# Two blocks of a transformer in one launch on one core: splits, waits and products reordered around three norms and at the last product

## The reference, cut to what matters

```python
x = x + hier_moe(rms_norm(x, ffn_norm), ...)           # 64 experts, top 2
h = rms_norm(x, final_norm)
xn = rmsnorm(h, pre_mix_norm)
rq, rk, rv, rg, cq, ckv, kr = split(xn @ w_in)
ret_out = silu(rg) * head_groupnorm(retention(rope(rq), rope(rk), rv), ret_gn_w)
q = rmsnorm(cq, mla_q_norm) @ w_uq; k, v = rmsnorm(ckv, mla_kv_norm) @ w_ukv   # MLA, 8 heads
mix = concat([ret_out, mla_causal(q, k, v)]) @ w_o
h = h + rmsnorm(mix, post_mix_norm)
ff = (silu(hn @ w_gate) * (hn @ w_up)) @ w_down        # hn = rmsnorm(h, pre_ffn_norm)
h = h + rmsnorm(ff, post_ffn_norm)
h = h + rmsnorm(p @ w_ple_proj, ple_norm) * sigmoid(h @ w_ple_gate + b_ple_gate)
```

## Time and profile before

| what | value |
|---|---|
| median of 3 runs | 2030.41 us (2029.95 to 2030.84) |
| the profiled execution, own time | 2028.34 us |
| its span | 2026.5 us |
| mean granted TensorE clock | 0.953 |
| PE, DVE, ACT, POOL busy | 87%, 45%, 32%, 13% |
| chain that ended last, by engine | PE 61%, DMA 28%, DVE 5%, ACT 2% |

### The profile page before, as it was taken

How to read it: one execution, slowest core, us unless ns; L and a number is a source line. 1 busy time by engine, 2 the same in 40 slices (tenths; PEclk the granted TensorE clock), 3 DMA queues, 4 the chain that set the end, 5 groups by cost and what they waited for, 6 DMA issues and landing times.

```text
span 2026.5 us, 37712 instructions
## 1 busy us (share of the span) xinstructions
PE 1758.4 (87%) x15176; PEld 1247.5 (62%) x15176; DVE 921.1 (45%) x1747; ACT 641.8 (32%) x1256; POOL 271.7 (13%) x285
## 2 busy tenths in 40 slices
PE   7999999887787787778778777789989899999998
PEld 5677788644343343434334343468867799998877
DVE  5455435332322232232223223375375698886245
ACT  4444522421111111111111111143365654445143
POOL 0000000000000000000000000640010078880000
PEclk9999999898998898898889889999999999999999
DMA  6222323799999999999999999943230233333222
GB/s 210 79 84 64 93 93 138 282 419 419 424 427 425 425 427 423 427 424 426 426 425 425 424 427 425 420 131 104 79 95 1 74 104 116 105 105 118 100 84 83
DMA packets 107012, 505.69 MB, mean 250 GB/s; under 512 B 7272, under 2 KB 56808, under 8 KB 73904
## 3 DMA queue, kind: packets, MB, share of 16 engines
q1 hardware_dynamic: 101184, 492.07, 61.0%
q10 hardware_dynamic: 3856, 7.74, 1.4%
q0 software_dynamic: 1888, 4.70, 0.9%
HBM read 496.80 MB, written 2.11 MB: 246 GB/s over the span
## 4 chain that ended last, share of the span: by engine, by line
PE 61%; DMA 28%; DVE 5%; ACT 2%; issue 2%; SPq 1%; ACTq 0%; POOLq 0%; DVEq 0%; POOL 0%
DMA ring<-in_w 27%; PE bank L704 13%; PE bank L705 13%; PE bank L706 13%; PE bank L2670 8%; PE bank L2599 4%; PE bank L2661 3%; PE bank L894 2%; PE bank L920 1%; PE bank L906 1%; SPq L2170 1%; PE bank L2683 1%; DMA raw<-in_w_in 1%; DVE w_split L811 1%; PE bank L1243 1%
## 5 line engine op out<-in xcount | busy, mean ns | idle before, releaser
L2670 PE MATMUL bank<-ring,XTs 128*32 128x256 f32 x3968 | 282.5, 433 | 144.1 <-DMA ring<-in_w 143.3
L2975 DVE TENSOR_TENSOR x<-x,bank 128x512 f32<-128x512 f32 x256 | 158.8, 682 | 493.3 <-PE bank L2661 493.2
L2670 PEld LDWEIGHTS bank<-ring,XTs 128*32 128x32 f32 x3968 | 142.2, 122 | 287.7 <-issue 236.4
L2683 PE MATMUL bank<-ring,aT 128*32 128x256 f32 x1984 | 119.9, 382 | 57.3 <-DVE aT L3002 57.3
L2428 ACT ACTIVATE y<-bank 32x256 f32<-32x256 f32 x254 | 95.1, 375 | 222.0 <-PE bank L2661 133.0
L704 PE MATMUL bank<-hT_all,w_split 128*128 128x512 f32 x362 | 148.2, 409 | 8.5 <-DVE w_split L811 3.1
L705 PE MATMUL bank<-hT_all,w_split 128*128 128x512 f32 x362 | 143.5, 396 | 0.0
L706 PE MATMUL bank<-hT_all,w_split 128*128 128x512 f32 x362 | 143.4, 396 | 0.0
L811 DVE TENSOR_TENSOR w_split<-raw,w_split 128x2048 fp32r<-128x2048 f32 (+4 forms) x46 | 96.0, 2093 | 98.8 <-ACT w_split L795 98.6
L2599 PE MATMUL bank<-arena,oh 128*32 128x256 f32 x2048 | 134.3, 404 | 6.0 <-DVE oh L2957 5.0
L2404 ACT ACTIVATE xe<-bank 128x256 f32<-128x256 f32 x64 | 24.5, 383 | 343.8 <-PE bank L2599 343.8
(11 more groups left out here) (483 smaller groups left out, 3641.6 us busy)
## 6 DMA issues: line engine op xcount, KB each, us to landing
ring<-in_w SPq DMA_DIRECT2D x186, 2048.0 KB, 19.9
raw<-in_w_in SPq DMA_DIRECT2D x24, 1024.0 KB, 5.5
late_raw<-in_w_gate SPq DMA_DIRECT2D x11, 1024.0 KB, 5.4
late_raw<-in_w_up SPq DMA_DIRECT2D x11, 1024.0 KB, 5.3
late_raw<-in_w_down SPq DMA_DIRECT2D x11, 1024.0 KB, 5.0
third<-in_w SPq DMA_DIRECT2D x4, 2048.0 KB, 11.8
raw<-in_w_out SPq DMA_DIRECT2D x4, 1024.0 KB, 5.1
raw<-in_w_o SPq DMA_DIRECT2D x4, 1024.0 KB, 5.2
```

The source lines that it names most:

```text
L2670: mm = pe.matmul(Hb[BLK * j:BLK * (j + 1), :], XTs[u][:, 4 * (c % 2) + 2 * h + c // 2, :], w[:, at_:at_ + Q], start=(h == 0 and c == 0), s ...
L2683: mm = pe.matmul(Yb[BLK * j:BLK * (j + 1), :], aT[:, r, h, :], w, start=(h == 0 and r == 0), stop=(h == 1 and r == 1))
L2975: ins = v.tensor_tensor(xs, xs, Sb[t % 2][n][:, :], ALU.add)
```

## The change

It has four places. **At the hand-over:** all banks are given back before the first product of u = 1; the first unit's splits move into u = 0 (DVE waits for `w_used` there); DVE splits the second unit before the variances; the rowscale matmul moves behind rk; POOL's scaling of x becomes one DVE operation for each tile behind the ropes, and ACT's first wait for x2 moves to the second latent stage. **At the start of attention:** gain and gate are multiplied in during retention (`gated_rows`), ACT drains mq_n2 and mq_n3 first and mk0, mk1 after the high parts, DVE takes the values in two portions around a weight split and the second rope turn inside attention; PE's waits for mv and ret_out move to first use. **At the second norm stage:** `om` starts with three of four chunks of two tiles; POOL makes the low parts of the first gate and up unit; the first transposes go ahead of the last `om` part, and the second half's ones into the middle of the first up product; the lists of DVE and ACT are reordered and the gain's DMA is issued earlier. **At the end:** all of ple goes ahead of the transposes.

```diff
         def loaded(pe, u):
-            pe.wait_ge(lo_made, u.count)
+            if u in ff_units[0:2]:
+                pe.wait_ge(S("first_lo"), ff_units.index(u) + 1)
+            else:
+                pe.wait_ge(lo_made, u.low)
...
         def pe_second(pe):
             pe_feature(pe, "rq", hT, fresh="hT3")
+            pe_feature(pe, "rk", hT)
             job = J["rowscale"][0]
...
             fill(pe.matmul(banks[job.bank][:, :], C("ones"), diag, start=True, stop=True), job)
-            pe_feature(pe, "rk", hT)
...
-            read(pe, J["mv"])
-            pe.wait_ge(S("ret_out"), RH)
             def pe_between():
+                pe.wait_ge(S("ret_out"), RH)
...
-            read(pe, J["mla_v"])
-            for i in range(NT):
-                for n in range(2):
...
+            for chunks in (range(3), (3,)):
+                for i in range(2):
+                    mla_part(i, 0, chunks)
+            mla_part(0, 1)
+            mla_part(1, 1)
+            mla_part(2, 0)
+            mla_part(2, 1)
+            mla_part(3, 0)
...
+                        if name == "up" and h == 0 and c == DC // 2:
+                            rows_to_columns(1)
...
+            rows_to_columns(0)
+            mla_part(3, 1)
             for h in range(2):
-                rows_to_columns(h)
                 first_pair(h)
...
             ple(0)
-            pe_to_feature(pe, J["hT5"], lambda i, c: x[:, i, P * c:P * (c + 1)], lambda i: pe.wait_ge(S("x4"), i + 1))
             ple(1)
+            pe.wait_ge(S("x4"), NT)
+            pe_to_feature(pe, J["hT5"], lambda i, c: x[:, i, P * c:P * (c + 1)])
...
         def dve_second(v, chain, evac):
+            v.wait_ge(S("angles"), ROPES["rope2"])
...
-            v.wait_ge(S("x2"), NT)
+            v.wait_ge(S("r3"), 1)
+            for i in range(NT):
+                v.scalar_tensor_tensor(x[:, i, :], x[:, i, :], rstd[:, i:i + 1], gain_fin, ALU.mult, ALU.mult).then_inc(S("x2"), 1)
...
+            def gated_rows(h):
+                read(v, J["ret_v"][h:h + 1])
+                v.scalar_tensor_tensor(rqT[:, h, :], rqT[:, h, :], PRM("ret_gn", h), rgT[:, h, :], ALU.mult,
+                                       ALU.mult).then_inc(S("ret_f"), 1)
...
+                if h:
+                    gated_rows(h - 1)
...
             for h in range(RH):
-                v.scalar_tensor_tensor(rqT[:, h, :], rqT[:, h, :], PRM("ret_gn", h), rgT[:, h, :], ALU.mult,
-                                       ALU.mult).then_inc(S("ret_f"), 1)
-                if h:
-                    dve_split(v, ("ret", h - 1), ...
+                dve_split(v, ("ret", h), osTl[:, h, :], rqT[:, h, :], osTh[:, h, :]).then_inc(S("ret_out"), 1)
...
+            values(0)
+            values(1)
             lo_until(v, units_of["or0"][0].n)
+            values(2)
+            values(3)
             def dve_between():
+                turned(1)
+                v.wait_ge(S("mq_roped"), 2)
...
+            lo_at.n = ff_units[1].n + 1
+            mixed(0, 0)
+            mixed(0, 1)
+            v.wait_ge(S("w_gm"), 16)
+            mix_gained(0)
+            mix_added(0)
+            mixed(1, 0)
+            mixed(1, 1)
+            n6.dve_mean(v, 0, ssq2, rstd2)
+            mix_gained(1)
...
-            read(act, J["ret_b"])
+            act.wait_ge(S("ret_f"), RH)
+            two_heads(J["mq_n"][2], mqT, 2, -(ML_QK ** -0.5))
+            two_heads(J["mq_n"][3], mqT, 3, -(ML_QK ** -0.5))
...
+            hi_until(act, ff_units[0].n)
+            act.activation(nsum, nsum, ACT.Sqrt)
+            squares_5(0)
+            n5.act_root(act, 0, rstd)
             hi_until(act, ff_units[1].n)
...
                     pe.wait_ge(xt_out, 2 * i + (u + 1))
+                    if u and last:
+                        given_back()
...
                     elif u == 0:
+                        if last:
+                            chain(v.tensor_tensor(mix_gain, ...))
+                            v.wait_ge(w_used, 2 * STEPS * i + STEPS)
+                            lo_at.limit = len(order)
+                            lo_until(v, n_first)
...
             dve_split_jobs(v, "hT3", hTh, hTl, lambda c: mix_gain[:, c:c + 1])
+            lo_until(v, n_first + 1)
...
-            pool.wait_ge(S("r3"), 1)
-            for i in range(NT):
-                chain(pool.tensor_tensor(xg(i), x[:, i, :], gain_fin, ALU.mult))
-                pool.tensor_scalar(x[:, i, :], xg(i), rstd[:, i:i + 1], None, ALU.mult).then_inc(S("x2"), 1)
...
+            for u in ff_units[0:2]:
+                pool.wait_ge(hi_made, u.count)
+                n = u.chunks * u.cols
+                pool.tensor_tensor(low(u, n), whole(u, n), high(u, n).bitcast(F32), ALU.subtract).then_inc(S("first_lo"), 1)
```

More of the change, by code:

```diff
@@ L427, in build @@
                 u.count = n_plain
+                u.low = n_plain - (2 if u.n > ff_units[1].n else 0)
         def high(u, n):
@@ L1052, in mla_step @@
                         added=lambda s: C("causal")[:, T - P * (i + 1):T],
-                        ready=lambda eng: mla_ready(p, eng))
+                        ready=lambda eng: mla_ready(p, eng), values=lambda eng: read(eng, J["mv"]))
         MLA = Attention("mla", pairs_of(mla_step), probs(av(10240, 1024), av(11264, 1024), av(12288, 1024)),
@@ L1329, in pe_second, with mla_part @@
                 pass
[L1330 to L1334 removed]
+            def mla_part(i, n, chunks=range(4)):
+                u, job, rows_ = units_of[f"om{n}"][0], J[f"om{n}"][i], slice(P * i, P * (i + 1))
+                wh, wl = parts(u)
+                if 0 in chunks:
                     loaded(pe, u)
[L1336 removed]
                     claim(pe, job)
[L1338 to L1341 removed]
+                for c in chunks:
+                    read(pe, J["mla_v"][c:c + 1])
+                    mm = three(pe, banks[job.bank][:, :], (catT[0](4 + c)[:, rows_], catT[1](4 + c)[:, rows_]),
+                               (wh[:, c, :], wl[:, c, :]), c == 0, c == 3)
+                if 3 in chunks:
+                    fill(mm, job)
+            for chunks in (range(3), (3,)):
[6 more added lines that the diff above has]
+            mla_part(3, 0)
             def rows_to_columns(h):
@@ L1677, in columns_lo, with mixed, mix_gained @@
                 ins.then_inc(S("op_lo"), 1)
-            lo_until(v, ff_units[0].n)
-            for i in range(NT):
-                for n in range(2):
-                    job, cols = J[f"om{n}"][i], slice(512 * n, 512 * (n + 1))
-                    full(v, job)
-                    read(v, J[f"or{n}"][i:i + 1])
-                    free(v.tensor_tensor(mixo[:, i, cols], mixg(i)[:, cols], banks[job.bank][:, :], ALU.add), job)
-                if i % 2:
-                    n6.dve_mean(v, i - 1, ssq2, rstd2)
-                if i == 2:
-                    columns_lo(0, 0)
-                    columns_lo(0, 1)
+            def mixed(i, n):
+                job, cols = J[f"om{n}"][i], slice(512 * n, 512 * (n + 1))
+                full(v, job)
+                read(v, J[f"or{n}"][i:i + 1])
+                free(v.tensor_tensor(mixo[:, i, cols], mixg(i)[:, cols], banks[job.bank][:, :], ALU.add), job)
+            def mix_gained(i):
                 read(v, [J["om0"][i], J["om1"][i]])
@@ L1977, in act_between @@
                         free(act.activation(mixg(i)[:, 512 * n:512 * (n + 1)], banks[job.bank][:, :], ACT.Copy), job)
+                        if n and i == NT - 1:
+                            row(gain_mix, "post_mix_norm_2", D, S("w_gm"))
                         yield
@@ L2414, in act_pair @@
                         gathered_out()
-                    if u and last:
-                        hi_at.limit = len(order)
-                        hi_until(act, n_first)
                     if u == 1:
@@ L2423, in act_pair @@
                                    ACT.Silu).then_inc(silu_out, 1)
+                    if last and u == 0:
+                        hi_at.limit = len(order)
+                        hi_until(act, n_first)
                     act.wait_ge(w_used, 2 * STEPS * i + STEPS * (u + 1))
@@ L2704, in rows_there, with given_back @@
                     pe.wait_ge(landed[3 * k + 2], 16 * n)
+            def given_back():
+                for job in J["before_moe"]:
+                    pe.sem_inc(filled[job.bank], 1)
+                    pe.sem_inc(freed[job.bank], 1)
             def pe_pair(i, last, buffers, first=False):
@@ L2792, in _ @@
             turned(2, 0, 4)
-            given_back(4, 6)
             for t in range(3):
```

122 lines of the change are left out of this document (58 added, 64 removed).

## The result

| | before | after |
|---|---|---|
| median of 4 runs | 2030.18 us | 2015.54 us (2014.17 to 2017.04) |
| ratio to before, 95% interval | | 0.9926 (0.9914 to 0.9937) |
| profiled execution, its span | 2028.34, 2026.5 us | 2014.17, 2012.4 us |
| mean granted clock | 0.953 | 0.954 |
| PE, DVE, ACT, POOL busy | 87%, 45%, 32%, 13% | 88%, 46%, 32%, 13% |

The forecast was 2015.8 us. To see whether it came out for the reasons given, I cut both executions at eight marks that are the same instruction in both programs, and took the differences of their starts.

What follows compares the result with a forecast made beforehand. Up to about 1317 us the experts' weight DMA bounds the kernel, behind that PE. Hand-over 7.9, attention 5.0, second norm stage -1.5 and end 3.2 sum to 14.6 us: from 2030.41 to 2015.8 us, range 2008.8 to 2021.2.

Steps and rivals of the forecast that it cites:

- Giving back: Hand-over: semaphore increments issued ahead of the last hidden product, first unit's split moved; gain 1.4 us (-1.4 to +1.6).
- The second unit's split: Hand-over: DVE splits the second weight unit before the square sums, so PE's gap and slow clock go; gain 6.5 us.
- rk's unit holds by 1 us: Hand-over: DVE's split of rk's first unit ends at 1351.3 us, PE asks at 1352.4; otherwise at most some 3 us lost.
- Scaling on DVE: Behind the ropes: POOL's scaling of x as four DVE operations of 1.28 us, 5.1 us in all, costs nothing.
- Attention: Start of attention: earlier drains and values remove PE's gaps and slow clock; gain 5.0 us (3 to 6).
- Second norm stage: From the mix product to the product at 1637.84 us: DVE waits for POOL, net -1.5 us (-4 to +4.5).
- POOL's lock: Second norm stage: DVE's multiplies wait for the whole of POOL's 4.8 us low parts, stretching to 4 and 6 us.
- POOL doesn't block DVE much: Rival for the second norm stage: stage gains 4.5 us, sum 20.6, total 2009.8 us; chance 0.22.
- the step that took the whole chain up to the first sum product as the end of the stage: Second norm stage: the whole chain up to the product at 1637.84 us comes out 1 to 2 us later.
- End: Transposes behind the whole embedding product: 24 matmuls cover both waits; gain 3.2 us (2.5 to 3.4).
- The Trainium skill's rule: Second norm stage: only DVE instructions with two SBUF inputs contend with GpSimd; without this half, -2.5 instead of -1.5 us.

Runs made afterwards that it cites:

- undo_norm: Changed kernel with the second norm stage's order and lists put back as before, both low parts on DVE again; 2012.50 us, ratio 0.9918.
- undo_end: Changed kernel with the transposes between the halves of the embedding product again; 2018.32 us, ratio 0.9939.
- lo_quarters: Changed kernel with each of POOL's two low parts cut into four operations of 512 columns; 2011.43 us, ratio 0.9912.
- quarters_high: Changed kernel with both the edits of lo_quarters and early_high; 2010.74 us, ratio 0.9896.
- early_high: Changed kernel with ACT's high part of each feed-forward unit's first four quarters waiting only for POOL's second sum; 2014.24 us, ratio 0.9920.

## Why the prediction was right, and where it wasn't

**Giving back: right** (1.4 us; 1.50 measured). The 1.42 us of issuing that it was read from are mostly the eight increments (1.2 us); the other 0.2 is the first unit's split.

**The second unit's split: right in size, too sure in its cause.** 6.5 us forecast, 6.60 measured. "rk's unit holds by 1 us" held: DVE's split ended at 1350.14 us, and PE came to rk's first product at 1351.2 without idle time. But the 3.0 us for the clock were put down as part of the gap's price. The runs show the gap at 3.4 us and the clock as a surcharge that isn't always due: a fair price would have been 3.4 to 6.5.

**Scaling on DVE: right.** Four operations in 4.86 us at 1401.38, and no idle time of PE behind them; not tested by itself.

**Attention: right.** 5.0 us forecast, 4.80 measured; the first or0 product 50.5 us after the first retention product (50.2 forecast), no stretch at 0.50. The reverse run confirms the place. Its edits came and went together, so that what each is worth isn't shown.

**Second norm stage: the mechanism right, the term too small.** POOL's lock was as forecast (its operations 0.2 us shorter; the multiplies 3.62 and 4.28 us for 4 and 6), and its rival ("POOL doesn't block DVE much", 0.22) is out: the multiplies at 1.22 us without POOL and 1.72 to 1.85 beside short pieces show it. The gap of 4.11 us (some 5 forecast) and the slow clock behind it came too. What failed is the step that took the whole chain up to the first sum product as the end of the stage and let everything behind it move along. Up to T it was better than forecast (+0.4 for -1.5), and then M, which the text never looked at, took 1.3 us, and the fallen clock behind it, with waits that followed, 2.4. In the kernel before the idle time of 2.23 us ahead of T covered a part of the chain that leads to M, and the slow clock between T and M the rest (0.17 us left there, 1.69 in undo_norm without that fall). With 0.80 us ahead of T that cover is gone. Whether it goes is not a matter of the order of work alone: in undo_end, where POOL came ahead of DVE by 0.08 us, 1.90 us of idle time stood ahead of T, and the stage lost 0.8 us rather than 3.2. Of A to D, -3.2 us in all lay within the bounds given (-4 to +4.5), and H's 1.2 us made up for it in the total. That the total came out within 0.3 us is luck to that extent.

**End: right** (3.2; 3.45).

The Trainium skill's rule in "SBUF — State Buffer", Who interferes with whom, was to change the sum by 1 us. Its half that no row had shown, that a DVE instruction with one SBUF input runs on beside GpSimd, holds here for the add with its second input in PSUM (0.69 us). It doesn't for every instruction with one: the tensor_scalar took 1.77 us instead of 0.75. The same section names DVE's two-port modes as a case that contends; the row is in accord with that, and the prediction's wording left it out.

## What to carry to other kernels

When a stage gets faster, find the next product whose operands come over another chain (here transfer, POOL, ACT, DVE), and work out that chain from its own start. Work handed to POOL should be cut into short instructions where DVE has two SBUF inputs: the waiting is by the instruction. Where both engines have such work at the same time, look at which comes first: here a difference of some 0.1 us went with 1.1 us of PE's idle time moving from one product to the next. And a gap of PE has two prices, its length and a chance of some us at the lower clock.

## What was not expected of the hardware

The granted clock behind a gap is not the same from one execution to the next. Ahead of M nine executions had a gap of 2.90 to 2.94 us: eight then fell to 0.50 for about 3.4 us, one (lo_quarters, 2.90 us) stayed at 1.00:

```profile
1630.00:1640.00 10.00, 8.73 (x72) 8.73 (x73) 8.58 (x11) 4.68 (x7) 9.77 (x6) 1.00 0.31 100
```

M to D is 193.87 to 196.06 us in the eight (1.4 to 3.6 more) and 192.46 in the one, as in those whose gap was 1.7 us or less. Behind T it fell with 2.23 us of idle time in the kernel before and with 1.97 in quarters_high, and not with 2.22 in undo_norm. Behind the 4.1 to 4.3 us ahead of the norm stage's transposes it fell each time, for 3.5 us once (early_high) and else for nearly 7. What decides between no fall, 3.4 us and nearly 7 stays open. What a fall costs depends on what follows. Between T and M of the kernel before it was nothing, since PE soon waits for another engine there. Behind M PE is the bound: in all eight executions that fell, the next unit's first product with T1 starts 14.5 to 14.6 us behind M, and 13.1 to 13.2 where the clock stayed, so that the fall itself cost 1.4 us. The rest, 0 to 2.1 us, is up to four short waits for DVE's low parts 50 to 115 us later, which the executions without a fall don't have.
